# Feed-forward products in rows of two rounded and two remainder tiles, in place of rows of eight

## The reference

```
def swiglu(x, w_gate, w_up, w_down):
    return (jax.nn.silu(x @ w_gate) * (x @ w_up)) @ w_down
...
for i in range(DEPTH):                                  # DEPTH = 2
    h = h + 0.5 * swiglu(rms_norm(h, norm_ff1[i]), ffn1_gate[i], ffn1_up[i], ffn1_down[i])
    h = h + mixer_i(rms_norm(h, norm_mix[i]))           # even: SSD and RG-LRU, odd: differential attention
    h = h + 0.5 * swiglu(rms_norm(h, norm_ff2[i]), ffn2_gate[i], ffn2_up[i], ffn2_down[i])
return rms_norm(h, final_norm)
```

## Time and profile before

| | |
|---|---|
| median of 3 runs | 1065.91 us (1065.07 to 1067.28) |
| the profiled execution | 1065.55 us |
| its span, first to last instruction | 1063.7 us |
| TensorE clock granted | 0.995 of full speed |
| PE busy / PEld busy | 1050.4 us (99%) / 944.8 us (89%) |
| DVE / ACT / POOL busy | 792.3 (74%) / 611.4 (57%) / 51.1 us (5%) |
| chain that ended last | PE 94%, of it L217 45% and L220 24% |
| transfers | 190.14 MB, mean 179 GB/s |

### The profile page before, as it was taken

How to read it: one execution, slowest core, us unless ns; L and a number is a source line. 1 busy time by engine, 2 the same in 40 slices (tenths; PEclk the granted TensorE clock), 3 DMA queues, 4 the chain that set the end, 5 groups by cost and what they waited for, 6 DMA issues and landing times.

```text
span 1063.7 us, 18486 instructions
## 1 busy us (share of the span) xinstructions
PE 1050.4 (99%) x6678; PEld 944.8 (89%) x6678; DVE 792.3 (74%) x1137; ACT 611.4 (57%) x980; POOL 51.1 (5%) x70
## 2 busy tenths in 40 slices
PE   9999999999999999999999999999999999999997
PEld 8888888899998998888888888888999998888886
DVE  6788776679868878887666888776699578888653
ACT  6555554468976665555445665543456756656541
POOL 0200011100000000000111000011100000000011
PEclk9999999999998999999999999999999999999999
DMA  8866775549644656667755666685566446667671
GB/s 250 213 195 193 211 205 162 156 124 259 175 114 125 200 156 191 189 194 206 208 158 159 196 196 189 197 218 165 146 169 165 120 127 200 190 195 204 188 200 40
DMA packets 369283, 190.14 MB, mean 179 GB/s; under 512 B 5920, under 2 KB 368704, under 8 KB 369232
## 3 DMA queue, kind: packets, MB, share of 16 engines
q1 hardware_dynamic: 368976, 188.89, 63.0%
q0 software_dynamic: 256, 0.59, 0.3%
HBM read 187.86 MB, written 1.07 MB: 178 GB/s over the span
## 4 chain that ended last, share of the span: by engine, by line
PE 94%; ACT 3%; DVE 2%; issue 1%; DVEq 0%; ACTq 0%
PE psum L217 45%; PE psum L220 24%; PE psum L201 7%; PE psum L205 7%; PE psum L202 6%; PE psum L1898 1%; ACT whi L185 1%; PE psum L1523 1%; DVE wlo L190 1%; PE psum L966 0%; DVE arena L1195 0%; PE psum L956 0%; PE psum L883 0%; PE psum L939 0%; PE psum L957 0%
## 5 line engine op out<-in xcount | busy, mean ns | idle before, releaser
L190 DVE TENSOR_TENSOR wlo<-raw,whi 128x1024 fp32r<-128x1024 f32 (+1 forms) x324 | 416.9, 1305 | 76.1 <-ACT whi L185 74.7
L185 ACT ACTIVATE whi<-raw 128x1024 fp32r<-128x1024 f32 (+1 forms) x324 | 354.0, 1113 | 35.0 <-PE psum L205 26.3
L217 PE MATMUL psum<-xn,whi 128*128 128x512 f32 x1408 | 354.3, 393 | 0.5 <-DVE xn L307 0.5
L217 PEld LDWEIGHTS psum<-xn,whi 128*128 128x128 f32 x1408 | 253.4, 189 | 46.7 <-issue 0.6
L220 PEld LDWEIGHTS psum<-xn,wlo 128*128 128x128 f32 x1408 | 192.4, 190 | 13.8
L220 PE MATMUL psum<-xn,wlo 128*128 128x256 f32 x1408 | 196.9, 282 | 0.0
L217 PE MATMUL psum<-hid,whi 128*128 128x512 f32 x704 | 171.8, 391 | 0.0
L217 PEld LDWEIGHTS psum<-hid,whi 128*128 128x128 f32 x704 | 128.1, 189 | 24.0
L201 PE MATMUL psum<-xn,whi 128*128 128x256 f32 x480 | 122.1, 292 | 0.9 <-ACT whi L185 0.9
L202 PE MATMUL psum<-xn,whi 128*128 128x256 f32 x480 | 118.9, 285 | 0.0
L510 ACT ACTIVATE arena<-arena 128x256 f32<-128x256 f32 x88 | 36.8, 419 | 112.4 <-DVE arena L574 112.4
(11 more groups left out here) (230 smaller groups left out, 873.1 us busy)
## 6 DMA issues: line engine op xcount, KB each, us to landing
raw<-in_ffn_gate SPq DMA_DIRECT2D x88, 512.0 KB, 3.9
raw<-in_ffn_up SPq DMA_DIRECT2D x88, 512.0 KB, 3.9
raw<-in_ffn_down SPq DMA_DIRECT2D x64, 704.0 KB, 4.6
raw<-in_hyb_w_in SPq DMA_DIRECT2D x36, 512.0 KB, 4.9
raw<-in_dif_w_qkv SPq DMA_DIRECT2D x24, 512.0 KB, 4.5
raw<-in_hyb_w_out SPq DMA_DIRECT2D x16, 512.0 KB, 4.7
raw<-in_dif_w_o SPq DMA_DIRECT2D x8, 512.0 KB, 4.1
hid<-cs_rows SPq DMA_DIRECT2D x4, 512.0 KB, 6.9
```

The lines of the kernel that those rows point to most:

```text
L185: act.activation(whi[:, s, 0:k * P], raw[:, s, 0:k * P], ACT.Copy).then_inc(s_whi, 1)
L190: dve.tensor_tensor(wlo[:, s, 0:k * P], raw[:, s, 0:k * P], whi[:, s, 0:k * P].bitcast(F32), ALU.subtract).then_inc(s_wlo, 1)
L217: pe.matmul(acc, hi[:, j, :], x[:, t, :, :], start=start and j == 0, stop=False)
```

## The change

`multiply_wide` now waits for both parts of the weights of a block before the first product, and issues the products in rows of two rounded tiles followed by the same two remainder tiles; a block of 11 ends with one of each, and so does a part of seven tiles. The number, shapes and operands of the products are the same, and so are their sums apart from the order. Nothing else is changed.

```
             hi, lo = tile_of(whi, s, k), tile_of(wlo, s, k)
             pe.wait_ge(s_whi, b + 1)
-            for j in part or range(k):
-                t = k0 + j
-                if need:
-                    need(t)
-                pe.matmul(acc, hi[:, j, :], x[:, t, :, :], start=start and j == 0, stop=False)
             pe.wait_ge(s_wlo, b + 1)
-            for j in part or range(k):
-                mm = pe.matmul(acc[:, T:2 * T], lo[:, j, :], x[:, k0 + j, 0, :], start=False,
-                               stop=stop and j == k - 1)
+            tiles = part or range(k)
+            for j0 in tiles[::2]:
+                two = [j for j in (j0, j0 + 1) if j in tiles]
+                for j in two:
+                    if need:
+                        need(k0 + j)
+                    pe.matmul(acc, hi[:, j, :], x[:, k0 + j, :, :], start=start and j == 0, stop=False)
+                for j in two:
+                    mm = pe.matmul(acc[:, T:2 * T], lo[:, j, :], x[:, k0 + j, 0, :], start=False,
+                                   stop=stop and j == k - 1)
             if j == k - 1:
                 mm.then_inc(s_blk, 1)
```

## The result

| | before | changed |
|---|---|---|
| median us (runs) | 1066.60 (4) | 1075.25 (4) |
| lowest to highest | 1065.07 to 1067.41 | 1074.58 to 1077.47 |
| profiled execution, us | 1065.55 | 1077.47 |
| its span, us | 1063.7 | 1075.7 |

The changed kernel is slower: ratio 1.0086, interval 1.0071 to 1.0100, some 9 us. The forecast was 1078 us with the range 1067 to 1086: the measured time lies in it and the sign is right. Its two terms did not fare alike.

A forecast was written before the change was run, and what follows sets the result against it. TensorE's product pitch was taken to bound the kernel, busy 99% of the span. 1065.55 us plus 8.6 for waits on wlo and 4.3 for changes of kind gave 1078.4, rounded to 1078, range 1067 to 1086.

The forecast's parts named there:

- Part 1: At block starts, TensorE waits for wlo, now needed earlier: 7.7 us of lateness plus 0.9 us of restarts, 8.6 us.
- seven stops: Program's first block, four first down blocks, second blocks of third and last feed-forward: wlo late by 0.85 to 1.22 us each.
- Elsewhere wlo is early: At all other blocks wlo is ready before TensorE, 0.99 us ahead in the tightest loop block, so loops wait for nothing.
- The term at the start: First block of the program: TensorE ready at 10.62, wlo at 11.84, so 1.22 us late.
- the restart: After each wait for wlo, TensorE loses an extra 0.13 us, 0.9 us for all 7.
- Part 2: Within blocks, switching between rounded and remainder products in short rows costs 1024c - 3.9 us, taken as +4.3 us.
- I take c = +0.008: Extra us for a row of two and two above 0.694, chosen nearer the heads of long rows; gives +4.3 us.
- One of the prediction's own signs of being wrong: Wrong if a block of 8 takes under 2.79 us, loops wait for wlo, or stops sum to under 5 us.
- Rival 2: Waits and register work make row heads dear, not changes of kind; block of 8 2.78 to 2.79, total 1070.3 to 1074.2 us; chance 0.20.
- Rival 1: Switching kinds within blocks is dearer, c +0.012 to +0.016: 1082.6 to 1086.7 us, block of 8 2.82 to 2.84; chance 0.23.
- Rival 3: Short rows gain as rounded products cover half the weight loads: 1060.1 us, block of 8 2.74 us; chance 0.09.
- Rival 4: VectorE's splits come earlier once TensorE is behind, halving the wait cost: 1074 us; chance 0.06.

The follow-up runs named there:

- e1: The kernel before with its long rows, only the wait for wlo moved ahead of each block's first product; 1075.90 us, ratio 1.0087.
- e5: The kernel before with rows of two in both loops, long rows with the late wait in the first four blocks of each; 1066.21 us, ratio 0.9989.
- e8: The kernel before with rows of one in the gate and up and down loops, long rows at the phase starts; 1073.62 us, ratio 1.0062.
- e3: The changed kernel with rows of one rounded and one remainder product, both waits in front; 1076.11 us (one run).
- e4: The changed kernel with rows of four and four, both waits in front; 1076.29 us (one run).
- e7: The kernel before with rows of one and one in the gate and up loop alone; 1071.45 us, ratio 1.0038.
- e11: The kernel before with rows of three in the gate and up loop, wlo waited for where first needed; 1066.22 us (one run).
- e10: Against the kernel before: rows of one in the gate and up loop, rows of two in each phase's first four blocks, late wlo wait; 1074.57 us (one run).
- e9: Against the kernel before: rows of one in all gate and up blocks, wlo wait behind the first rounded product, long down rows; 1066.66 us (one run).
- e12: Against the kernel before: rows of one from each feed-forward's third gate and up block on, wlo wait where first needed, long rows elsewhere; 1062.69 us, ratio 0.9966.

## Why the prediction was right, and which step was off

**Part 1, right in place, a little small in size.** The seven stops came where the starts and the ends of L190 had put them, and e1 shows that they are the loss. One small stop was missed: "Elsewhere wlo is early" was too generous at the first block of the last feed-forward, where 0.11 us of lead was not enough and 0.15 us was lost. Measured from block to block, against the kernel before: 1.1 us at the program's start, 4 x 1.46 in the down blocks, 1.31 in the third feed-forward, 0.93 and 0.15 in the last, 9.3 us in all against 8.6 forecast.

The term at the start is the least certain. The first product comes 1.26 us later than in the kernel before, and the fourth block 1.08. But in the traces without this stop (e5 to e8) the first product starts anywhere from 10.50 to 11.53 us, against 10.62 before. In the changed kernel's own execution the last warm-up product starts at 11.21 and they follow each other every 0.216, so without the wait the first product would have come near 11.43 and not at 10.62 (an estimate), and the wait alone holds it for some 0.45 us.

The mis-sized term is the restart: 0.13 us a stop was taken, and the down blocks show 1.46 - 1.12 = 0.34 us each, 0.26 of it from the end of L190 to the product and 0.07 behind it; the second blocks of the third and last feed-forward show 0.19 and 0.08. The weight load itself is not what takes the 0.26: the product starts 0.03 us after its load does, and the time lies between the end of L190 and the load. Why that is 0.23 us in a down block and 0.12 at the two second blocks stays open. That the third down block's wlo is covered by the first stop held: no wait stands there.

**Part 2, wrong in size and sign.** The step that failed is "I take c = +0.008". With 2.787 and 3.840 us, c is (2.787 - 2.776) / 4 = +0.003 in blocks of 8 and (3.840 - 3.817 - 0.003) / 5 = +0.004 in blocks of 11, and part 2 comes to about -0.6 us (160 x -0.0066, 60 x +0.0075) in place of +4.3. So 1065.55 + 9.3 - 0.6 = 1074.3 us beside the measured 1075.25; the forecast was 4.9 too high in part 2 and 0.7 too low in part 1. One of the prediction's own signs of being wrong came true: a block of 8 takes under 2.79 us. The total was close because part 1, the larger term, was nearly right and part 2 is small beside the range, not because part 2 was understood.

Finer readings would not have saved it. The 10 ns resolution leaves anything from -0.004 to +0.016 for 0.47 + 0.23 against 0.694, but in ns the head of a long row runs 233, 236, 113, 119, sum 701, which is +0.008 again. What failed is to price a short row by the head of a long one: in the changed kernel the rows take turns between 233, 236, 116, 112 and 233, 231, 113, 119, sums 697 and 696. And a price for each change of kind was the wrong form: e3, e4, e7 and e11 show that the sum depends on which repeating pattern of pitches the sequence falls into.

**The rivals.** Rival 2 had the number for the block (2.78 to 2.79) but its reason, waits at the head, is refuted by e1 and by the rows inside a block. Rival 1 is out by the block. Rival 3's gain does not come in rows of two; rows of one have one of 0.020 us a block in the fast cadence, so its sign is shown possible, and its mechanism (cover for the weight loads) was not tested. Rival 4 is out: VectorE's splits did not come earlier (L190 of the first down block starts 2.3 us after the block before it, as in the kernel before).

Rival 2 took the rule of the Trainium skill in "TensorE: Matmul & The Clock Gate", part 2, step 1, that the weights of the next tile load while this one's matmul runs, to mean that order is nothing. The overlap itself is in the profile: 942.6 us of weight loads beside 1055.4 us of products in a span of 1075.7. What was drawn from it is not: the same products take 2.773 to 2.827 us a block of 8 by order and by history.

## What to carry to other kernels

A wait moved ahead of work in an in-order queue costs its lateness wherever the producer is just in time, so compare the two sides' times block by block, phase starts above all: here 8 of 240 blocks made the whole loss, one of them with its operand done 0.11 us ahead. Place a wait directly before the first instruction that needs it. Where a loop is bound by TensorE's pitch, read the block time over dozens of blocks; a difference of some ns for each product is worth more than it looks, and can only be tried.

## What the runs showed of the hardware

The same loop of alternating 512- and 256-column fp32r products runs in one of two stable cadences, 2.773 or 2.827 us for 16 products at a granted clock of 1.00, and keeps it for all 40 blocks of a phase, through the loop's own branches and waits. After blocks in long rows or rows of two it was the slow one (e7, e8, e10: 12 loops of 12); after two blocks in rows of one, just behind the sums of squares (L385), the fast one in 11 loops of 12 (e3, e9, e12). The exception, the third feed-forward of e3, had its first two blocks in the slow cadence, but so had the first feed-forward of e3, whose loop was fast. Each count is of one traced execution for each kernel. What holds the cadence, and what in the products before the loop selects it, stays open: it was seen, not explained.
